# Second norm of a decoder layer: squares and transposes taken per column group, row scale applied last and spread over partitions by TensorE

## What is computed

```python
h = rms_norm(x, norm1_w[l]) * (1.0 + sc1) + sh1
proj = h @ w_in[l]
...
y_mix = jnp.concatenate([y_attn, y_rec], axis=-1) @ w_out[l]
x = x + g1 * y_mix

h = rms_norm(x, norm2_w[l]) * (1.0 + sc2) + sh2
u = causal_depthwise_conv(h @ w_up[l], conv_w[l], conv_b[l])
gate, up = u[..., :D_FF], u[..., D_FF:]
x = x + g2 * ((jax.nn.silu(gate) * up) @ w_down[l])
```

## Time and profile before

| what | value |
|---|---|
| median of 3 runs | 1374.73 us (1373.86 to 1375.15) |
| the profiled execution, its own time | 1364.12 us |
| its span in the trace | 1362.2 us |
| mean granted TensorE clock | 0.965 |
| PE busy | 1225.5 us, 90% |
| PEld busy | 1074.8 us, 79% |
| DVE busy | 1024.4 us, 75% |
| ACT busy | 588.4 us, 43% |
| 16 DMA engines, main queue | 67.0% |

### The profile page before, as it was taken

The page is one execution under the profiler, slowest core; times in us unless marked ns, Lnnn a source line. Parts: engine busy times, 40 slices in busy tenths (PEclk is TensorE's granted clock), DMA queues, the critical chain, the costliest instruction groups (busy, mean ns, idle before and its releaser), DMA issues.

```text
span 1362.2 us, 20195 instructions
## 1 busy us (share of the span) xinstructions
PE 1225.5 (90%) x7005; PEld 1074.8 (79%) x7005; DVE 1024.4 (75%) x1261; ACT 588.4 (43%) x741; POOL 55.9 (4%) x103
## 2 busy tenths in 40 slices
PE   0108999999999999959999999999999999999995
PEld 0108999899998877848888888888888878888884
DVE  5997888878878788757878888898868765545543
ACT  2104444444545554444444444444444434333332
POOL 3000000012022000000000000000000000000000
PEclk9657999999999999979999999999999999999998
DMA  9894987767769879746777677767555575555551
GB/s 374 347 416 137 391 313 263 244 225 246 234 208 302 303 263 385 258 145 226 247 243 239 234 244 232 234 231 243 186 189 193 186 262 193 193 195 193 185 201 77
DMA packets 138623, 329.71 MB, mean 242 GB/s; under 512 B 10693, under 2 KB 11446, under 8 KB 133570
## 3 DMA queue, kind: packets, MB, share of 16 engines
q1 hardware_dynamic: 134592, 316.71, 67.0%
q0 software_dynamic: 3424, 10.00, 2.1%
q10 hardware_dynamic: 546, 2.20, 0.4%
HBM read 323.09 MB, written 4.19 MB: 240 GB/s over the span
## 4 chain that ended last, share of the span: by engine, by line
PE 86%; DVE 6%; DMA 3%; ACT 2%; issue 2%; ACTq 0%; DVEq 0%; SPq 0%
PE bank L979 24%; PE bank L981 12%; PE bank L1002 6%; PE bank L1003 6%; PE bank L1004 6%; PE bank L780 5%; PE bank L782 5%; PE bank L781 5%; PE bank L766 5%; PE bank L769 4%; PE bank L768 4%; DMA astart<-in_w_ada 3%; DVE acc L1076 2%; PE bank L812 1%; PE bank L797 1%
## 5 line engine op out<-in xcount | busy, mean ns | idle before, releaser
L1144 DVE TENSOR_TENSOR wlo<-wraw,whi 128x1024 fp32r<-128x1024 f32 x404 | 493.6, 1223 | 282.0 <-ACT whi L527 279.7
L527 ACT ACTIVATE whi<-wraw 128x1024 fp32r<-128x1024 f32 x408 | 431.9, 1060 | 626.1 <-PE bank L981 238.8
L979 PE MATMUL bank<-h,whi 128*128 128x512 f32 x1408 | 488.7, 394 | 2.0 <-DVE wlo L1144 1.9
L981 PE MATMUL bank<-h,wlo 128*128 128x256 f32 x1408 | 390.1, 277 | 0.0
L979 PEld LDWEIGHTS bank<-h,whi 128*128 128x128 f32 x1408 | 264.0, 188 | 63.9 <-DVE wlo L1144 2.2
L981 PEld LDWEIGHTS bank<-h,wlo 128*128 128x128 f32 x1408 | 264.2, 188 | 0.0
L766 PE MATMUL bank<-h,whi 128*128 128x256 f32 x512 | 149.2, 291 | 4.9 <-DVE wlo L1144 4.4
L769 PE MATMUL bank<-h,wlo 128*128 128x256 f32 x512 | 146.7, 287 | 0.0
L768 PE MATMUL bank<-h,whi 128*128 128x256 f32 x512 | 146.7, 286 | 0.0
L1002 PE MATMUL bank<-whi,act_hi 128*128 128x512 f32 x352 | 137.0, 389 | 0.3 <-DVE evt L1335 0.3
L1003 PE MATMUL bank<-wlo,act_hi 128*128 128x512 f32 x352 | 136.9, 389 | 0.0
(11 more groups left out here) (203 smaller groups left out, 1215.8 us busy)
## 6 DMA issues: line engine op xcount, KB each, us to landing
wraw<-in_w_up SPq DMA_DIRECT2D x176, 512.0 KB, 3.5
araw<-in_w_ada SPq DMA_DIRECT2D x128, 512.0 KB, 5.0
wraw<-in_w_in SPq DMA_DIRECT2D x112, 512.0 KB, 4.1
wraw<-in_w_down SPq DMA_DIRECT2D x88, 512.0 KB, 3.5
astart<-in_w_ada SPq DMA_DIRECT2D x32, 1024.0 KB, 7.2
wraw<-in_w_out SPq DMA_DIRECT2D x32, 512.0 KB, 5.6
x<-in_x ACTq DMA_DIRECT2D x1, 2048.0 KB, 18.6
x<-in_x POOLq DMA_DIRECT2D x1, 2048.0 KB, 12.3
```

The source lines that it names most:

```text
L527: act.activation(whi[:, slot], wraw[:, slot], ACT.Copy).then_inc(s_hi, 1)
L979: pe.matmul(out, whi[:, slot, k, cols], h[:, kk].rearrange("p a t -> p (a t)"), start=(kk == 0), stop=False, skip_group_check=True)
L981: last = pe.matmul(out[:, 0:SEQ], wlo[:, slot, k, cols], h[:, kk, 0, :], start=False, stop=(kk == KT - 1), skip_group_check=True)
L1144: dve.tensor_tensor(wlo[:, slot], wraw[:, slot], whi[:, slot].bitcast(F32), ALU.subtract).then_inc(s_lo, 1)
```

## The change

The squares are taken per column group and token block as soon as `out_columns` has written it (`x1_squares`, 128 by 512, eight sums in `ssg`). TensorE transposes the unscaled `x1` of that group (`x1_transposes`), and ACT copies the result to SBUF (`x1_columns`, tile `x1T`). Groups 0 to 2 do this within the output projection, two steps (transposes) and four steps (copies) after their `out_columns`; group 3 behind it. A square root on a spare column at step 141 has the table loaded early. At the end DVE adds the eight sums to two, ACT takes the root, DVE the reciprocal `r` and the two diagonal matrices `diag = ident * r`; TensorE multiplies `ones` by them, which puts `r[t]` on every partition, in bank 4. Then `htmp = x1T * A2 * r`, with `B2` added in the two instructions that write `h`. DVE's and ACT's split of the up units 4 to 7 moves from `ffn_half` into the loop over the tiles.

```diff
+OUT_AT = (OUT0 + 10, OUT0 + 17, OUT0 + 25)
...
+            def x1_squares(g, b):
+                act.wait_ge(s_x1, 2 * g + b + 1)
...
+                act.activation(x1sq[:], x1[:, b, g * UW:(g + 1) * UW], ACT.Square, accum_out=ssg[:, b, g:g + 1]).then_inc(s_x1sq, 1)
+
+            def x1_columns(g):
+                for q in range(2):
+                    act.wait_ge(s_x1T, 2 * g + q + 1)
+                    act.activation(x1T[:, 4 * g + 2 * q:4 * g + 2 * q + 2, :],
+                                   ps[4 + 2 * (g % 2) + q].rearrange("p (a t) -> p a t", a=2), ACT.Copy).then_inc(s_x1Tc, 1)
...
-            norm_sums(x1, junk)
-            h_hi(1)
+                for g in range(3):
+                    if s == OUT_AT[g] + 1:
+                        x1_squares(g, 0)
+                        x1_squares(g, 1)
+                    elif s == OUT_AT[g] + 4:
+                        x1_columns(g)
+                if s == UP0 - 3:
+                    act.activation(spare, epsc, ACT.Sqrt).then_inc(s_spre, 1)
+
+            x1_squares(3, 0)
+            x1_squares(3, 1)
+            act.wait_ge(s_ssum, 1)
+            act.activation(rstd, ss, ACT.Sqrt, bias=epsc, scale=1.0 / D).then_inc(s_rt, 1)
+            x1_columns(3)
+            for k in range(KT):
+                act.wait_ge(s_ht, KT + k + 1)
+                act.activation(h[:, k, 0, :], htmp[:, k % 2], ACT.Identity, bias=B2[:, k:k + 1]).then_inc(s_hhi, 1)
+                if k % 2 and k >= 9:
+                    v = UP0 + RING + (k - 9) // 2
+                    hi_part(v % RING, (v // RING + 1) * 16, v - RING + 1)
...
+            def x1_transposes(g):
...
+                for b in range(TB):
+                    pe.wait_ge(s_x1, 2 * g + b + 1)
+                    for k in range(4):
...
+                for g in range(3):
+                    if s == OUT_AT[g] + 2:
+                        x1_transposes(g)
...
-            x_transposes(xn, 1, 0, 4)
+            x1_transposes(3)
+            pe.wait_ge(s_x1Tc, 6)
+            for b in range(TB):
+                pe.wait_ge(s_diag, b + 1)
+                last = pe.matmul(ps[4][:, b * P:(b + 1) * P], ones[:], diag[:, b], start=True, stop=True)
+            last.then_inc(s_row, 1)
...
+            dve.wait_ge(s_x1sq, 8)
+            dve.tensor_reduce(ss, ssg, AX.X, ALU.add).then_inc(s_ssum, 1)
+            dve.wait_ge(s_rt, 2)
+            st.then(dve.reciprocal(ss, rstd))
+            for b in range(TB):
+                dve.tensor_scalar(diag[:, b], ident[:], ss[:, b:b + 1], None, ALU.mult).then_inc(s_diag, 1)
+
+            dve.wait_ge(s_row, 1)
...
+                    dve.scalar_tensor_tensor(out=htmp[:, k % 2], in0=x1T[:, k, :], scalar=A2[:, k:k + 1], in1=ps[4][:, 0:SEQ],
+                                             op0=ALU.mult, op1=ALU.mult).then_inc(s_ht, 1)
...
+                    dve.scalar_tensor_tensor(out=h[:, k - 1, 1, :], in0=htmp[:, (k - 1) % 2], scalar=B2[:, k - 1:k],
+                                             in1=h[:, k - 1, 0, :].bitcast(F32), op0=ALU.add, op1=ALU.subtract).then_inc(s_h, 1)
+                if k >= 10 and k % 2 == 0:
+                    v = UP0 + RING + (k - 10) // 2
+                    lo_part(v + 1, v % RING, v - RING + 1)
```

More of the change, by code:

```diff
@@ L557, in _ @@
             act.activation(cosr[:], cosr[:], ACT.Sin).then_inc(s_cs, 1)
[L558 to L567, removed]
+            for k in range(KT):
+                act.wait_ge(s_ht, k + 1)
+                act.activation(h[:, k, 0, :], htmp[:, k % 2], ACT.Copy).then_inc(s_hhi, 1)
+                if k % 2 and k // 2 < AHEAD:
+                    act.wait_ge(s_ada, 2 * KT + 4)
+                    hi_part(k // 2, 16)
             def evacuate(n):
@@ L722, in _ @@
             last.then_inc(s_prmT, 1)
[L724 to L736, removed]
-            pe.wait_ge(s_xn, 1)
-            x_transposes(x0, 0)
+            pe.wait_ge(s_xn, 1)
+            for k in range(KT // 2):
+                if k >= 4:
+                    pe.wait_ge(s_xTc, k - 3)
+                for a in range(2):
+                    for b in range(TB):
+                        last = pe.transpose(ps[4 + k % 4][:, a * SEQ + b * P:a * SEQ + (b + 1) * P],
+                                            x0[:, b, (2 * k + a) * P:(2 * k + a + 1) * P], ident[:])
+                last.then_inc(s_xT, 1)
             def mod_columns(a, col, k0, k1, bank0):
@@ L771, in channel_unit, with token_unit @@
                 last.then_inc(s_pe, 1)
-            def token_unit(n, j, hi, lo, tiles):
+            def token_unit(n, j, hi, lo, tiles, early=None):
                 slot = j % RING
@@ L782, in token_unit @@
                         last = pe.matmul(out, lo(kk, tok), whi[:, slot, k, :], start=False, stop=end)
+                    if early and b == 0:
+                        last.then_inc(early, 1)
                 last.then_inc(s_pe, 1)
@@ L1251, in out_columns @@
                 dve.wait_ge(s_g1, 2 if g < 2 else 4)
-                dve.wait_ge(s_pe, OUT0 + 8 * g + 8)
                 for b in range(TB):
                     cols = slice(g * UW, (g + 1) * UW)
-                    st.wait()
+                    if g == 3 and b == 0:
+                        dve.wait_ge(s_outb, 1)
+                    else:
+                        dve.wait_ge(s_pe, OUT0 + 8 * g + 8)
+                    if g or b:
+                        dve.wait_ge(s_x1, 2 * g + b)
                     dve.tensor_tensor(ytmp[:], ps[g % 2 * 2 + b], g1b[:, cols], ALU.mult).then_inc(s_evac, 1)
                     dve.wait_ge(s_evac, 2 * g + b + 1 + 4)
-                    st.do(dve.tensor_tensor(x1[:, b, cols], x1[:, b, cols], ytmp[:], ALU.add))
+                    dve.tensor_tensor(x1[:, b, cols], x1[:, b, cols], ytmp[:], ALU.add).then_inc(s_x1, 1)
             dve.wait_ge(s_lvm, 1)
```

127 lines of the change are left out of this document (74 added, 53 removed).

## The result

| | kernel before | changed kernel |
|---|---|---|
| median | 1374.79 us (22 runs) | 1362.2 us (22 runs) |
| lowest to highest | 1366.03 to 1375.9 | 1360.75 to 1372.51 |
| lower level, mean | 1366.31 (4 runs) | 1361.91 (15 runs) |
| upper level, mean | 1374.79 (18 runs) | 1371.25 (7 runs) |
| profiled execution: time, span | 1364.12, 1362.2 | 1362.31, 1360.3 |

The ratio is 0.9943, 95% interval 0.9925 to 0.996. It is not the ratio of the two medians, which would be 0.9908: the means of all executions differ by 8.4 us. The kernel is 12.6 us faster at the median; forecast were 3.7 us, 1371.0, in a range from 1368.0 to 1373.2. So the sign was right and the size wrong.

What follows compares the result with a forecast made beforehand. TensorE was taken as the bound, except in the open stretch between output and up projection. Unit 8 8.1 us earlier, less 4.4 for transposes, gave 3.7 us less: 1360.4 profiled, 1371.0 with the 10.6 us difference, range 1368.0 to 1373.2.

Steps and rivals of the forecast that it cites:

- The chain: Between output and up projection: first up matmul 11 us after the projection's last, where it was 17.7.
- the two products: Ahead of the up projection: two multiplications of `ones` by the diagonals, 0.44 us each.
- a tile: Tile loop ahead of and beside the first up units: 1.05 us each, where it was 0.98.
- The clock: At the first up units: half-speed work on the clock's ramp loses 1.65 to 3.05 us, taken as 2.35.
- Transposes in the projection: Groups 0 to 2 inside the output projection: added TensorE time of 1.73, 1.78 and 0.88 us, 4.4 in sum.
- The sum: Whole kernel: 8.1 us gained by unit 8 less 4.4 for transposes in the projection, 3.7 us less.
- From profile to median: Whole kernel: the runs' median stays 10.6 us above the profiled execution, so 1360.4 becomes 1371.0 us.
- the stretch: Between output and up projection, where TensorE idles from 594.45 to 607 us; time taken out comes off the total.
- The 1.88 us wait goes: Up unit 4: TensorE no longer waits 1.88 us for `wlo`, with 2 to 3 us to spare.
- The clock is kept: Rival, between the projections: short work holds or raises the clock, no 2.35 us loss; gain 6.0, 1368.7 us; chance 0.15.
- A longer chain: Rival, between the projections: slower hand-overs, longer ramp and waits; gain 1.8, time 1372.9 us; chance 0.25.
- DVE turns the projection slower: Rival, output projection: squares delay DVE, TensorE waits for `out_columns`; up to 3.8 us slower, 1378.5; chance 0.04.

Runs made afterwards that it cites:

- e1_late: The changed kernel with the transposes of column groups 0 and 1 one step later; median 1360.33 us, ratio 0.9924 to the kernel before.
- e3_after_order: The changed kernel with each up-projection unit's two 512-column matmuls ahead of its two 256-column ones; median 1363.99 us, ratio 0.9941 to the kernel before.
- e2_order: e1_late with the up projection's four matmuls per output grouped, two of 512 columns, then two of 256; median 1362.25 us, ratio 0.9923 to the kernel before.
- e3_before_order: The kernel before with each up-projection unit's two 512-column matmuls ahead of its two 256-column ones; median 1368.04 us, ratio 0.9963 to the kernel before.
- e2_break: e1_late with one single-column product ahead of each of the 22 up-projection groups; 1369.01 us in one execution.

## Why the forecast was wrong

**The chain.** Right. Forecast were 11.1 us from the projection's last matmul to the first up matmul, measured 11.2. Single terms were off and cancelled: the square with its sum 0.72 us (0.73 forecast), reduction with its hand-over 0.20 (0.25), root and reciprocal 0.53 (0.54), the two products 1.20 (0.88), a tile 0.94 (1.05). (The second norm has 32 blocks of 128 by 128, not 64 as the section on the kernel before says; the forecast counted records, so its sum is not touched.)

**The clock.** Right as a middle value. The ramp was taken as the middle of 3.3 and 6.1 us; in this trace it lasted 6.0, the upper end. From first up matmul to unit 8 it took 25.0 us, of which 64 pairs at 0.347 are 22.2; so 2.8 us were lost here, not 2.35, and unit 8 gained 7.8 us instead of 8.1. Counted the same way the loss is 2.4 us in e1_late, 2.5 in e3_after_order and 1.6 in e2_order, and the seven ramps have a mean of 4.8 us, so 2.35 describes the executions better than the one trace does.

Here the clock stayed at half through transposes and products with gaps, where the earlier trace rows has it rise behind dense transposes. By the rule of the Trainium skill (page "TensorE: Matmul & The Clock Gate", section "PE-mode transpose") that transposes do not count, the new trace would be explained and the old one not. No run here separates the kind of work from its density.

**Transposes in the projection.** Right: 1.73, 1.73 and 0.88 us against 1.73, 1.78 and 0.88, with a gap inside the first two (0.63 and 0.64 us, 0.8 forecast) and none in the third. Removing the gaps gave back what their terms said (e1_late).

**The sum.** 7.8 - 4.3 = 3.5 by the marks of the trace, with its long ramp; 3.7 forecast. Runs say 4.05 (grouped order), and 3.95 and 3.5 on the lower and the upper level against the pooled executions of before (1365.86 and 1374.79). The traces' spans differ by only 1.9 us, since the changed kernel reached the output projection 1.4 us later in its trace. The whole of that arose between 385 and 404 us, far ahead of the change, where its trace has TensorE at half clock from 394.2 to 397.6, behind a wait of 2.31 us, and the trace of before has the same wait and no fall of the clock (windows of the changed kernel, then of before):

```profile
394.00:398.00 4.00, 4.00 (x22) 3.89 (x21) 3.35 (x6) 0.00 (x0) 0.00 (x0) 0.57 0.79 261
```

```profile
394.00:398.00 4.00, 4.00 (x34) 3.95 (x34) 3.44 (x6) 0.50 (x1) 0.00 (x0) 1.00 0.75 259
```

Eight of the 14 profiles have this fall, e3_before_order among them, so it is a difference between executions and not of the change. It costs 1.5 us where it comes.

**From profile to median.** This step failed: "The median of the runs is 10.6 us above it; nothing in the stretch depends on that, so I take the difference over as it is". Both halves were false. Of the 10.6 us, 8.9 were the distance of two levels, and 1.7 that the profiled execution was quicker than the mean of the lower one. And the stretch did have a say in it: the share of the levels moved with the split of units 4 to 7, an edit that the forecast itself prices ("The 1.88 us wait goes"), and in the traces the spacing turned long at the stop which that edit removes. With two levels and a median, the shares are worth more than the work saved: about 4 us on each level, and 9 us for each execution that goes from one to the other. That the sign came out right owes nothing to this step.

**The rivals.** *The clock is kept*: fell, it was at half for 13.7 us, from 602.4 to 616.0; but as an edit it brings 2.4 to 2.9 us. *A longer chain*: the ramp came at its long end in this trace, the hand-overs did not. *DVE turns the projection slower*: did not occur; TensorE never waited for the whole of `out_columns`. The true rival, a second spacing of the same instructions, was not listed. Both spacings stood in the one profile, 353 ns in unit 0 and 347 in unit 2, though nothing in it said that the whole phase could run at the longer one; that was only in the distance between the profile's own time and three runs that agreed.

## What to carry to other kernels

When the profiled execution lies further from the median than the runs scatter, it is an execution of another kind: find what differs before a difference is carried over, and list every execution rather than the median. In a long stream of alternating long and short matmuls compare the distance between starts across executions; if it has two values, group equal sizes together, which here gave one level near the lower one and pays where most executions are on the upper, or try to keep waits out of the place where the stream begins. A single trace also has a clock history of its own: look at the granted clock of both traces before two spans are compared. Transposes put among matmuls should stand one step behind the data they wait for, and a mostly idle stretch of TensorE of some 10 us before a dense phase is worth filling.

## What the hardware showed unasked

- Pairs of a 512- and a 256-column matmul, each with its own weight load, ran 346.7 or 353.3 ns apart, with the same instructions, at the same clock. At full clock the value changed only at interruptions, down to one single-column product. At half clock a pair took 640 ns.
- In e2_break the value changed at every group from the third to the last of 22, long and short in turn.
- Two long, then two short gave one level in all 32 executions of four kernels, at 348 ns a pair.
- The clock came back 3.3 to 6.0 us after the first up matmul behind sparse work (seven traces), 3.3 us after dense transposes began.
- After the same wait of 2.31 us near 391 to 394 us the clock fell in eight of 14 profiles and stayed up in six.
- ACT's high part with an added column took 0.51 us, the plain copy 0.416.
